# The first stage of a two-block model as one list of steps

## The chip, the cores and the metric

One core of a Trainium2 chip runs the whole program in one launch. The metric is the device time in microseconds. Before the change it is 3861.12 us, the median of three runs from 3858.9 to 3863.61. All data is fp32.

## What is computed

Two model blocks work on x of 256 rows by 2048. Block one is an attention layer and a Fourier layer, each behind a modulated layer norm; block two is a mixer, a cross-attention to a memory of 256 rows, and an expert layer with gathered rows. The change touches only the first stage, which prepares three things:

```
# modulation of layer 0, for the latents (c) and the context (c_ctx)
m = silu(cvec) @ ada_w[0] + ada_b[0]          # 2048 -> 6144; shift, scale, gate
h = layer_norm(x) * (1 + scale) + shift        # for x with c, for ctx with c_ctx
# keys and values of the memory
mem_n = rms_norm(mem, mem_norm_g)
kv = mem_n @ w_kv_mem                          # 2048 -> 4096: 2048 keys, 2048 values
```

Shift and scale, the first 4096 columns, are needed in this stage; the gate's columns come later. h of x and of ctx then goes into attention's input product (`z = h @ w_in`), whose first part is called z_q. Keys and values wait in DRAM for the second block.

## The kernel before, in words

Each engine has its own generator of instructions: `sp_mem`, `pe_mem`, `v_mem`, `a_mem` for the first stage (SP issues the loads, PE is TensorE, v is VectorE or DVE, a is ScalarE or ACT), then `sp_attention` and so on. Weights come through a ring of eight units of 1 MiB (`sp_slot`): a load waits until what was in its unit has been used. Beside its main work a program has a side list; `aside` (L98) takes steps from it at a rate, after each chunk of weights. SP, PE, DVE and ACT must take side steps at the same places, since they are written to meet there.

The order before is this. Constants arrive, ACT and DVE compute S5 phases (`a_phases`, `v_phases`), while POOL builds tables from them all the way to 723 us. Memory's rows are normed, turned by PE (L602) and evicted as columns by DVE (L621) and ACT (L637). Then the key blocks run (`pe_cols`, L354: four blocks of 512 columns, 16 k-steps of 128 each, plain fp32), and the value blocks (`pe_rows`, L331: plain fp32, 512 wide). Beside them run, at 3.2 steps for a chunk of eight k-steps, eight modulation blocks of 512 columns (`v_modulation`). For each of the 16 k-steps and each of the two vectors, DVE multiplies a row block of `ada_w` by a scalar of each partition and adds it up (L814); PE then sums over partitions with 8 matmuls against a column of ones (L841), and DVE adds the bias (L823). There is one pair of sums, `macc`: the next block can't begin until PE has read it, and DVE waits for that at L823 in its own order. Last come x and ctx, from the ring: DVE computes row moments (L690) and DVE and ACT norm one tile of 128 rows each (L697, L706); PE turns the rows in four parts of four k-steps (L602); DVE and ACT evict with scale and shift (L623, L639), ACT makes the high part (L441) and DVE the low part (L447).

Attention's products are split products in fp32r: a weight is a high part plus a low part, and so is the input; three fp32r matmuls (L470, L471, L472) stand for one fp32 matmul. For each k-step ACT copies the high part of the weights (L419) and DVE subtracts for the low one (L431), into four buffers (`BUFS`), which lie in the ring's last two units; `sp_parts` takes these from the ring and `a_parts` waits for them. In `split`, ACT and DVE are three k-steps ahead of the eviction and the side steps of a k-step. Behind the first stage the side list is the row modulation, the other 16 blocks (L874, L877).

Of the kernel before, what the change touches and what calls it, by code (L numbers as in the profile page):

```python
# [13 lines left out]
P = 128  # L14
# [357 lines left out]


def v_rows_out(c, L, tiles, dst):

    for b, (n, w) in enumerate(L.blocks):
        for _ in L.chunks[:-1]:
            yield from c.v.aside()
        for q, t in enumerate(tiles):
            if (b * len(tiles) + q) % 2 == 0:  # L380
                key = (L.name, n, t)
                yield from v_copy_out(c, key, dst(t, n, w), lambda: c.bank[key][:, 0:w])
        yield from c.v.aside()


def a_rows_out(c, L, tiles, dst):
    for b, (n, w) in enumerate(L.blocks):
        for _ in L.chunks[:-1]:
            yield from c.a.aside()
        for q, t in enumerate(tiles):  # L390
            if (b * len(tiles) + q) % 2:
                key = (L.name, n, t)
                yield from a_copy_out(c, key, dst(t, n, w), lambda: c.bank[key][:, 0:w])
        yield from c.a.aside()
# [186 lines left out]
def first_load(L):  # L581
    return (L.name, L.n0, 0)
# [198 lines left out]
def mod_load(layer, n, ch):  # L781
    return ("ada", layer, n, ch)


def sp_modulation(c, layer, blocks):
    W = c.I["ada_w"][layer]
    for n in blocks:
        for ch in range(2):
            yield from sp_load(c, mod_load(layer, n, ch),
                               W[ch * 8 * P:(ch + 1) * 8 * P, n:n + 512].rearrange("(k p) n -> p k n", p=P), 8, 512)  # L790
            yield True
            yield True
        yield True


def v_modulation(c, layer, blocks, who):
    nc, v = c.nc, c.v
    for n in blocks:
        for kk in range(KD):
            load = mod_load(layer, n, kk // 8)  # L800
            if kk % 8 == 0:
                yield from v.wait_ge(("in", load))
                wt = c.slot(load, 8, 512)
            elif kk % 4 == 0:
                yield True
            for w in range(who):
                acc, cv = c.macc[:, w, :], c.cv[:, w, kk:kk + 1]
                names = [("macc", layer, n, kk, w)]
                names += [("used", load)] if kk % 8 == 7 and w == who - 1 else []
                if kk == 0:  # L810
                    nc.vector.tensor_scalar(acc, wt[:, 0, :], cv, None, ALU.mult).then_inc(c.v_mod.after(*names), 1)
                else:
                    yield from v.wait_ge(("macc", layer, n, kk - 1, w))
                    nc.vector.scalar_tensor_tensor(out=acc, in0=wt[:, kk % 8, :], scalar=cv, in1=acc, op0=ALU.mult,  # L814
                                                   op1=ALU.add).then_inc(c.v_mod.after(*names), 1)
            if kk % 8 == 7:
                yield True
        key = ("mod", layer, n)
        yield from v.wait_ge(("full", key))
        j = n // P  # L820
        m = c.mod[:, layer, j:j + 4, 0:who]
        scale = D <= n < 2 * D
        nc.vector.tensor_tensor(m, c.bank[key][:, 0:4 * who].rearrange("p (a b) -> p a b", b=who),  # L823
                                c.col("ada_b%d" % layer)[:, j:j + 4].unsqueeze(2).broadcast_to([P, 4, who]),
                                ALU.add).then_inc(c.v_mod.after(("free", key), *([] if scale else [key])), 1)
        if scale:
            yield from v.wait_ge(c.v_mod)
            nc.vector.tensor_scalar(m, m, 1.0, None, ALU.add).then_inc(c.v_mod.after(key), 1)
        yield True


def pe_modulation(c, layer, blocks, who):
    for n in blocks:
        for _ in range(4):
            yield True
        key = ("mod", layer, n)
        bank = yield from pe_bank(c, c.aux, key)
        yield from c.pe.wait_ge(*[("macc", layer, n, KD - 1, w) for w in range(who)])
        for j in range(4):
            for w in range(who):  # L840
                mm = c.nc.tensor.matmul(bank[:, j * who + w:j * who + w + 1], c.macc[:, w, j * P:(j + 1) * P],  # L841
                                        c.ones[:, 0:1], start=True, stop=True)
        mm.then_inc(c.pe_full.after(("full", key)), 1)
        yield True


# [184 lines left out]

def mem_lins(c):
    W = c.I["w_kv_mem_2"][0]
    return Lin("mem_k", W, 0, D), Lin("mem_v", W, D, 2 * D)


def mem_views(c):
    return c.at(16 * K1, KD, SEQ), c.at(20 * K1, NT, D), c.at(24 * K1, KD, SEQ)


MOD0A = range(0, 2 * D, 512)
MOD0B = range(2 * D, 3 * D, 512)
MOD1 = range(0, 3 * D, 512)
INPUTS = (("x", 0), ("ctx", 1))
# [12 lines left out]

def pe_mem(c):
    pe = c.pe
    LK, LV = mem_lins(c)  # L1060
    KT, VV, memT = mem_views(c)
    mem = c.ring[:, 0, :].rearrange("p (t d) -> p t d", t=NT)
    yield from pe.wait_ge(("const", "rope"))
    yield from pe_turn(c, "mem", lambda k, t: mem[:, t, k * P:(k + 1) * P], KD, NT, normed("mem"))
    c.moments[("used", "mem")] = c.moments[("full", turn_banks("mem", KD, NT)[-1][0])]
    pe.side, pe.rate = [pe_modulation(c, 0, MOD0A, 2)] + [pe_input(c, name) for name, _ in INPUTS], 3.2
    yield from pe.wait_ge(*turn_free("mem", KD, NT))
# [6 lines left out]
def v_cols_out(c, L, dst, beside=True):  # L1074

    for n, w in L.blocks:
        if beside:
            for _ in L.chunks[:-1]:
                yield from c.v.aside()
        for j in range(0, w // P, 4):  # L1080
            key = (L.name, n, j)
            yield from v_copy_out(c, key, dst((n - L.n0) // P + j), lambda: pairs(c.bank[key][:, :]))
        if beside:
            yield from c.v.aside()


def a_cols_out(c, L, dst, beside=True):
    for n, w in L.blocks:
        if beside:
            for _ in L.chunks[:-1]:  # L1090
                yield from c.a.aside()
        for j in range(2, w // P, 4):
            key = (L.name, n, j)
            yield from a_copy_out(c, key, dst((n - L.n0) // P + j), lambda: pairs(c.bank[key][:, :]))
        if beside:
            yield from c.a.aside()


def v_mem(c):
    v = c.v  # L1100
    LK, LV = mem_lins(c)
    KT, VV, memT = mem_views(c)
    mem = c.ring[:, 0, :].rearrange("p (t d) -> p t d", t=NT)
    yield from v.wait_ge(("const", "rope"))
    yield from v_phases(c)
    yield from v.wait_ge(("in", "mem"))
    yield from v_rms(c, "mem", ("mem", "squares"))
    v_rms_rows(c, "mem", lambda t: mem[:, t, :], lambda t: mem[:, t, :])
    yield from v_turn_out(c, "mem", lambda k: memT[:, k, :], KD, NT, gain=lambda k: c.col("memn_g", k))
    yield from v.wait_ge(("mem", "silu"))  # L1110
    v.side, v.rate = [v_modulation(c, 0, MOD0A, 2)] + [v_input(c, name, w) for name, w in INPUTS], 3.2
    yield from v_cols_out(c, LK, lambda j: KT[:, j:j + 2, :])
    yield from v_rows_out(c, LV, range(NT), lambda t, n, w: VV[:, t, n - D:n - D + w])
    yield from v.aside(0)
    v.side = [v_row_modulation(c)]
# [28 lines left out]
def sp_input(c, name):  # L1144
    yield from sp_load(c, ("rows", name), c.I[name][0].rearrange("(t p) d -> p t d", p=P), NT, D)
    yield True
    for _ in range(4):
        yield True
# [1910 lines left out]
```

## Time and profile before

| | us |
|---|---|
| median of the runs | 3861.12 |
| the profiled execution, time | 3859.63 |
| its span | 3858.3 |
| busy PE / DVE / ACT / POOL | 2783.1 / 2677.6 / 1011.8 / 1491.3 |
| first matmul of the keys / of z_q | 28.10 / 334.61 |

PE is TensorE's matmuls, PEld its weight loads, DVE VectorE, ACT ScalarE, POOL GpSimd, SP the queue that issues the loads. A line number is that of the instruction, often a helper's. "Idle before" is the time that an engine stood still ahead of an instruction, and "<-" names what it waited for. The granted clock (PEclk) is TensorE's, with 1.00 for 2.4 GHz. A plain fp32 matmul appears as two records.

### The profile page before, as it was taken

What the parts mean: (1) busy time and instruction counts of PE and PEld (TensorE: products, weight loads), DVE (VectorE), ACT (ScalarE), POOL (GpSimd) and SP (SyncE); (2) the same over time, 40 slices, a digit from 0 to 9 for tenths busy, and PEclk for the clock granted to TensorE, in tenths of its full rate; (3) what the DMA queues carried; (4) which work ended last, traced back from release to release, by engine and by line L of the source; (5) the groups of instructions that cost most, each with busy time, mean ns of one, the idle gap of its engine ahead of it and who ended that gap; (6) DMA issues with size and microseconds to landing.
All of it is one profiled execution on the core that took longest, in us unless ns stands there. A gap on an engine that the chain in (4) does not pass through costs nothing.

```text
span 3858.3 us, 34052 instructions
## 1 busy us (share of the span) xinstructions
PE 2783.1 (72%) x12628; PEld 2060.6 (53%) x12628; DVE 2677.6 (69%) x3883; ACT 1011.8 (26%) x1884; POOL 1491.3 (39%) x1943
## 2 busy tenths in 40 slices
PE   7897989878799998979997897832434444444445
PEld 6645888546688975859876796730111111111112
DVE  6766867786654432657884554679888878888775
ACT  1013334123444421444465543410000000000000
POOL 7887877300000000000000000047776767777664
PEclk9888999999899999989998998865676766676678
DMA  8767666745455520544212451369999999999998
GB/s 295 267 240 250 222 241 213 254 137 182 153 192 187 184 88 22 187 173 164 99 66 92 159 219 66 134 255 405 417 421 422 421 421 411 417 421 419 420 422 343
DMA packets 284166, 974.23 MB, mean 253 GB/s; under 512 B 13408, under 2 KB 29664, under 8 KB 214752
## 3 DMA queue, kind: packets, MB, share of 16 engines
q0 software_dynamic: 76592, 551.58, 34.7%
q1 hardware_dynamic: 206000, 413.79, 30.4%
q10 hardware_dynamic: 1408, 6.69, 0.4%
q8 instruction: 99, 1.62, 0.2%
q14 instruction: 67, 0.55, 0.0%
HBM read 957.33 MB, written 14.68 MB: 252 GB/s over the span
## 4 chain that ended last, share of the span: by engine, by line
PE 53%; DVE 19%; DMA 15%; POOL 7%; issue 3%; ACT 3%; SPq 0%; DVEq 0%; ACTq 0%
DMA ring<-in_peer_v,arena 11%; POOL ring L2926 7%; PE lin L470 6%; PE lin L471 6%; PE lin L472 6%; PE lin L505 5%; PE lin L2690 5%; PE lin L508 5%; PE lin L507 5%; DVE mod_sums L877 3%; DMA ring<-in_peer_u,arena 3%; PE lin L2103 3%; DVE mod_sums L814 2%; PE lin L354 2%; DVE ring L2847 2%
## 5 line engine op out<-in xcount | busy, mean ns | idle before, releaser
L2690 PE MATMUL lin<-ring,diag 128*128 128x512 f32 x768 | 531.7, 857 | 738.7 <-DMA ring<-in_peer_v,arena 572.4
L431 DVE TENSOR_TENSOR weight_parts<-ring,weight_parts 128x512 fp32r<-128x512 f32 (+2 forms) x1010 | 660.9, 672 | 491.1 <-ACT weight_parts L419 489.4
L419 ACT CAST weight_parts<-ring 128x512 fp32r<-128x512 f32 (+2 forms) x1010 | 596.3, 598 | 748.5 <-PE lin L472 421.7
L2690 PEld LDWEIGHTS lin<-ring,diag 128*128 128x128 f32 x768 | 206.2, 282 | 1059.3 <-issue 883.2
L2847 DVE CUSTOM_DVE_ANT_0 ring<-ring,arena 128x2048 f32<-128x2048 f32 x256 | 583.4, 2289 | 156.8 <-DMA ring<-in_peer_u,arena 148.5
L2926 POOL DMA_INDIRECT ring<-in_peer_u,arena x256 | 458.9, 1793 | 421.8 <-DVE arena L2781 273.3
L2926 POOL DMA_INDIRECT ring<-in_peer_v,arena x256 | 467.7, 1827 | 234.9 <-PE lin L2690 161.6
L470 PE MATMUL lin<-weight_parts,parts 128*128 128x512 f32 (+2 forms) x1252 | 483.2, 386 | 57.6 <-DVE weight_parts L431 55.9
L2451 POOL DMA_DIRECT2D arena<-mem_values x1 | 0.6, 567 | 1347.5 <-PE lin L508 1347.5
L505 PE MATMUL lin<-parts,weight_parts 128*128 128x256 f32 x1600 | 465.7, 291 | 52.5 <-DVE weight_parts L431 52.5
L471 PE MATMUL lin<-weight_parts,parts 128*128 128x512 f32 (+2 forms) x1252 | 479.2, 383 | 0.0
L472 PE MATMUL lin<-weight_parts,parts 128*128 128x512 f32 (+2 forms) x1252 | 478.4, 382 | 0.0
L508 PE MATMUL lin<-parts,weight_parts 128*128 128x256 f32 x1600 | 461.0, 288 | 0.0
L507 PE MATMUL lin<-parts,weight_parts 128*128 128x256 f32 x1600 | 461.0, 288 | 0.0
L2835 DVE SCALAR_TENSOR_TENSOR arena<-ring,arena 128x2048 f32<-128x2048 f32 x160 | 375.9, 2349 | 49.4 <-DMA ring<-in_peer_v,arena 47.0
L505 PEld LDWEIGHTS lin<-parts,weight_parts 128*128 128x128 f32 x1600 | 316.2, 198 | 60.7 <-DVE weight_parts L431 54.7
L507 PEld LDWEIGHTS lin<-parts,weight_parts 128*128 128x128 f32 x1600 | 316.2, 198 | 0.1
L508 PEld LDWEIGHTS lin<-parts,weight_parts 128*128 128x128 f32 x1600 | 315.6, 197 | 0.0
L470 PEld LDWEIGHTS lin<-weight_parts,parts 128*128 128x128 f32 x1252 | 239.8, 192 | 110.4 <-DVE weight_parts L431 56.6
L472 PEld LDWEIGHTS lin<-weight_parts,parts 128*128 128x128 f32 x1252 | 239.6, 191 | 44.8
L471 PEld LDWEIGHTS lin<-weight_parts,parts 128*128 128x128 f32 x1252 | 239.7, 191 | 43.4
L2900 ACT ACTIVATE diag<-ident,arena 128x128 f32<-128x128 f32 x96 | 35.0, 394 | 609.3 <-PE lin L2690 489.8
(274 smaller groups left out, 3561.2 us busy)
## 6 DMA issues: line engine op xcount, KB each, us to landing
ring<-in_ada_w SPq DMA_DIRECT2D x64, 1024.0 KB, 6.5
ring<-in_w_in_fourier SPq DMA_DIRECT2D x32, 2048.0 KB, 8.0
ring<-in_w_kv_mem SPq DMA_DIRECT2D x16, 2048.0 KB, 10.9
ring<-in_ada_w SPq DMA_DIRECT2D x16, 2048.0 KB, 8.1
ring<-in_w_in_attn SPq DMA_DIRECT2D x32, 1024.0 KB, 6.9
ring<-in_w_out_fourier SPq DMA_DIRECT2D x16, 2048.0 KB, 8.0
ring<-in_w_in SPq DMA_DIRECT2D x24, 1024.0 KB, 5.1
ring<-in_w_out_attn SPq DMA_DIRECT2D x8, 2048.0 KB, 7.9
```

The source lines that it names most:

```text
L419: c.nc.scalar.copy(c.w_parts[:, q, 0, 0:w], c.slot(load, L.kc, w)[:, k % L.kc, :]).then_inc(c.a_high.after(("high", L.name, i)), 1)
L431: c.nc.vector.tensor_tensor(c.w_parts[:, q, 1, 0:w], c.slot(load, L.kc, w)[:, k % L.kc, :], c.w_parts[:, q, 0, 0:w].bitcast(F32), ALU.subt ...
L470: c.nc.tensor.matmul(banks[t][:, 0:w], lhs(0, k, t), hi, start=(k == 0), stop=False)
L471: c.nc.tensor.matmul(banks[t][:, 0:w], lhs(0, k, t), lo, start=False, stop=False)
L472: mm = c.nc.tensor.matmul(banks[t][:, 0:w], lhs(1, k, t), hi, start=False, stop=(k == L.K - 1))
L505: c.nc.tensor.matmul(o, hi[:, b], rhs(0, k), start=(k == 0 and j % 2 == 0), stop=False, skip_group_check=True)
L507: c.nc.tensor.matmul(o, hi[:, b], rhs(1, k), start=False, stop=False, skip_group_check=True)
L508: mm = c.nc.tensor.matmul(o, lo[:, b], rhs(0, k), start=False, stop=(k == L.K - 1), skip_group_check=True)
L2690: mm = nc.tensor.matmul(X.sums[t][b][:, :], c.diag[:, X.diag_of(t, k), :], X.bufs[gather_buf(n)][:, b * 512:(b + 1) * 512], start=(k == PE ...
L2835: nc.vector.scalar_tensor_tensor(out=X.H[:, t, :], in0=X.bufs[gather_buf(n)], scalar=X.act[:, t, k:k + 1], in1=X.H[:, t, :], op0=ALU.mult, ...
L2847: c.nc.vector.tensor_tensor_reduce(out=buf, in0=buf, in1=X.hn[:, t, :], scale=1.0, scalar=0.0, op0=ALU.mult, op1=ALU.add, accum_out=X.act[ ...
L2926: c.nc.gpsimd.indirect_dma_start(X.bufs[q], None, X.tables[table], bass.IndirectOffsetOnAxis(ap=X.idx[:, t, k:k + 1], axis=0)).then_inc(go ...
```

## The change

The side work of the first stage becomes one list, `beside_memory`, of 45 steps, which all four engines walk. There are 32 modulation steps (4 blocks of 1024 columns, each in 8 loads of two k-steps, 1 MiB), two norms (x behind the 16th modulation step, ctx behind the last), two pauses for the last sums, eight input parts and an end. There are two pairs of sums, and PE reads a pair two steps after its last addition, DVE adds the bias three steps after. The four additions of a step alternate between the two vectors, as before. Three steps are taken ahead of the keys (DVE one ahead of memory's rms, two behind it), 1.44 a chunk of four k-steps in the keys and 1.25 in the values. ACT takes over all evictions of keys, values and inputs and all of the inputs' normalising; DVE keeps the row moments and the low parts. Memory's values become split products; their input parts are made from memory's columns, the high part in other space and the low part in place, so DVE waits for the last key block. x's rows are loaded by SP ahead of the keys, ctx's rows by ACT's queue when the keys are stored, both into the arena and not the ring. The values leave in four stores of a block each. `sp_parts` and `a_parts` move ahead of the values. DVE's phases and ACT's first activation wait only for the first constants, whose order changes, and ACT's silu comes ahead of the phases.

```diff
-    return Lin("mem_k", W, 0, D), Lin("mem_v", W, D, 2 * D)
+    return Lin("mem_k", W, 0, D, kc=4, rate=1.44), Lin("mem_v", W, D, 2 * D, kc=4, every=4, rate=1.25)
...
+        self.KT = c.at(16 * K1, KD, SEQ)
+        self.T, self.T_flat = c.at(24 * K1, KD, SEQ), c.at(24 * K1, KD * SEQ)
+        self.parts = [c.at_r(20 * K1, KD * SEQ), c.at_r(24 * K1, KD * SEQ)]
+        self.V = c.at(28 * K1, 2, NT, 512)
+        self.x = [c.at(8 * K1, NT, D), c.at(16 * K1, NT, D)]
+        self.sums = [c.at((12 + 2 * i) * K1, 2, MOD_WIDTH) for i in range(2)]
...
+    steps = [("mod", b, q) for b in range(2 * D // MOD_WIDTH) for q in range(KD // 2)]
+    steps.insert(16, ("norm", 0))
+    steps += [("norm", 1), ("sum",), ("sum",)] + [("part", w, q) for w in range(2) for q in range(4)] + [("last",)]
...
+def v_beside(c):
+    nc, v, X, steps = c.nc, c.v, c.mem_in, beside_memory()
+    due, low = mod_due(steps, 3), None
...
+            yield from v.wait_ge(("in", load))
+            wt = c.slot(load, 2, MOD_WIDTH)
+            for k in range(2):
+                for w in range(2):
...
+                    else:
+                        yield from v.wait_ge(("sum0", b, q - (k == 0), 1 - k, w))
+                        nc.vector.scalar_tensor_tensor(out=acc, in0=wt[:, k, :], scalar=cv, in1=acc, op0=ALU.mult,
+                                                       op1=ALU.add).then_inc(c.v_mod.after(*names), 1)
+        if s[0] == "norm":
+            yield from v_input_norm(c, s[1])
...
+        if i in due:
+            yield from v_modulated_both(c, due[i])
+        yield True
...
+def a_beside(c):
...
+        if s == ("mod", 3, 3):
+            yield from a.wait_ge(("memk", "stored"))
+            nc.scalar.dma_start(X.x[1], c.I["ctx"][0].rearrange("(t p) d -> p t d", p=P)).then_inc(
+                Signal(c, "ctx_rows_in", 16).after(("rows", "ctx")), 16)
+        if s[0] == "norm":
+            w, name = s[1], INPUTS[s[1]]
+            yield from a_rstd(c, name, st_tmp(c, NT))
+            yield from a.wait_ge(("bias", name))
...
 def sp_mem(c):
...
-    sp.side, sp.rate = [sp_modulation(c, 0, MOD0A)] + [sp_input(c, name) for name, _ in INPUTS], 3.2
+    sp.side = [sp_beside(c)]
+    yield from sp.aside(3)
+    c.nc.sync.dma_start(c.mem_in.x[0], c.I["x"][0].rearrange("(t p) d -> p t d", p=P)).then_inc(
+        Signal(c, "x_rows_in", 16).after(("rows", "x")), 16)
+    sp.owed = 0.0
     yield from sp_weights(c, LK)
+    sp_parts(c)
     yield from sp_weights(c, LV)
...
 def pe_mem(c):
...
-    yield from pe_cols(c, LK, lambda k: memT[:, k, :])
-    yield from pe_rows(c, LV, lambda k, t: memT[:, k, t * P:(t + 1) * P], range(NT))
+    pe.side, pe.owed = [pe_beside(c)], 0.0
+    yield from pe.aside(3)
+    begin(pe, LK)
+    yield from pe_cols(c, LK, lambda k: X.T[:, k, :])
+    yield from pe_split_rows(c, LV, ("mem",), X.lhs)
...
 def v_mem(c):
...
+    yield from v_phases(c)
+    yield from v.wait_ge(("mem", "silu"))
+    v.side, v.owed = [v_beside(c)], 0.0
+    yield from v.aside(1)
...
+    yield from v.aside(2)
+    begin(v, LK)
+    for _ in LK.blocks:
+        for _ in LK.chunks:
+            yield from v.aside()
+
+    def x_part(q):
+        yield from v.wait_ge(("full", (LK.name, LK.blocks[-1][0], 2)))
+        yield from v_low_of_x(c, "mem", q, X.T_flat, *X.parts)
+
+    yield from v_split(c, LV, x_part, nothing)
...
 def a_mem(c):
...
+    yield from a_parts(c, first_load(LV))
+    yield from a_split(c, LV, None, out)
```

## Rows read from the trace of the kernel before

**Rows 1.** The page: its chain of waits by engine, whole span.

```profile
PE 53%; DVE 19%; DMA 15%; POOL 7%; issue 3%; ACT 3%; SPq 0%; DVEq 0%; ACTq 0%
```

**Rows 2.** Stretches: us, busy of each engine (instructions), PEclk, DMA share, GB/s.

```profile
28.00:335.00 307.00, 263.55 (x961) 179.55 (x962) 215.42 (x343) 29.14 (x46) 246.85 (x628) 0.90 0.67 244
```

**Rows 3.** Who waited for whom, 0 to 335 us: total us, times, longest.

```profile
DVE mod L823 <- PE aux L841: 30.7, 8, 7.9
...
PE aux L841 <- DVE mod_sums L814: 24.9, 5, 9.6
...
PE aux L602 <- DVE ring L697: 11.8, 1, 11.8
```

**Rows 4.** The PE's timeline: start, us, what, count, idle before it.

```profile
28.10 27.86 PE L354 MATMUL lin<-arena,ring 128*128 128x256 f32 x128 [1.13 <-ACT arena L637]
...
110.56 3.54 PE L841 MATMUL aux<-ones,mod_sums 128*128 128x1 f32 x16 [9.59 <-DVE mod_sums L814]
113.97 29.95 PE L354 MATMUL lin<-arena,ring 128*128 128x256 f32 x128
...
279.28 2.87 PE L602 MATMUL aux<-ident,ring 128*128 128x128 f32 x24
281.98 13.90 PE L331 MATMUL lin<-ring,arena 128*128 128x512 f32 x32
...
334.61 0.79 PE L470 MATMUL lin<-weight_parts,parts 128*128 128x512 f32 x1 [6.57 <-DVE weight_parts L431]
335.20 0.63 PE L471 MATMUL lin<-weight_parts,parts 128*128 128x512 f32 x1
335.62 0.63 PE L472 MATMUL lin<-weight_parts,parts 128*128 128x512 f32 x1
...
344.32 0.39 PE L471 MATMUL lin<-weight_parts,parts 128*128 128x512 f32 x1
344.55 0.39 PE L472 MATMUL lin<-weight_parts,parts 128*128 128x512 f32 x1
```

**Rows 5.** The DVE's timeline.

```profile
17.37 0.16 DVE L731 TENSOR_REDUCE st<-square_sums 128x2 f32<-128x8 f32 x1 [4.59 <-ACT squares_out L717]
...
204.68 19.96 DVE L814 SCALAR_TENSOR_TENSOR mod_sums<-ring,silu_c,mod_sums 128x512 f32<-128x512 f32 x30
...
263.06 4.83 DVE L690 BATCH_NORM_STATS2 bn<-ring 128x6 f32<-128x512 f32 x8
...
282.92 1.23 DVE L447 TENSOR_TENSOR parts<-arena,parts 128x1024 fp32r<-128x1024 f32 x1 [2.00 <-ACT parts L441]
...
333.77 2.71 DVE L431 TENSOR_TENSOR weight_parts<-ring,weight_parts 128x512 fp32r<-128x512 f32 x4
```

**Rows 6.** ACT's timeline.

```profile
282.79 1.01 ACT L639 ACTIVATE arena<-aux,mod 128x256 f32<-128x256 f32 x2
...
307.53 2.93 ACT L706 ACTIVATE ring<-ring,st 128x512 f32<-128x512 f32 x4 [1.43 <-DVE st L693]
...
331.55 1.04 ACT L441 CAST parts<-arena 128x1024 fp32r<-128x1024 f32 x1 [1.28 <-DVE arena L623]
...
337.62 0.62 ACT L419 CAST weight_parts<-ring 128x512 fp32r<-128x512 f32 x1 [2.51 <-PE lin L472]
```

**Rows 7.** Costliest groups by shape: busy us, mean ns, idle before.

```profile
L2835 DVE SCALAR_TENSOR_TENSOR arena<-ring,arena 128x2048 f32<-128x2048 f32 x160 | 375.9, 2349 | 49.4 <-DMA ring<-in_peer_v,arena 47.0
...
L1455 DVE TENSOR_TENSOR arena<-arena 128x1024 f32<-128x1024 f32 x2 | 3.0, 1490 | 0.1
```

**Rows 8.** Stretches under load, columns as in rows 2.

```profile
350.00:360.00 10.00, 10.00 (x49) 8.41 (x48) 9.51 (x16) 4.25 (x9) 3.56 (x13) 1.00 1.05 374
360.00:370.00 10.00, 7.42 (x60) 7.01 (x58) 8.40 (x17) 4.63 (x12) 8.74 (x25) 1.00 0.93 314
```

**Rows 9.** DMA issues of the first 340 us: count, KB each, median us to landing.

```profile
mem_keys<-arena ACTq DMA_DIRECT2D x1, 2048.0 KB, 11.6
```

**Rows 10.** POOL's timeline, first stage over.

```profile
894.48 0.72 POOL L1754 DMA_DIRECT2D arena<-in_x  x1 [170.85 <-DVE arena L1548]
```

More of the change, by code:

```diff
@@ L775, in pe_spread @@
         yield True
[L781 to L829, printed above, removed]
@@ L832, in pe_modulation @@
[L832 to L844, printed above, removed]
@@ new lines, in pe_beside @@
+def pe_beside(c):
+    X, steps = c.mem_in, beside_memory()
+    due = mod_due(steps, 2)
+    for i, s in enumerate(steps):
+        if i in due:
+            b = due[i]
+            key = ("mod0", b)
+            bank = yield from pe_bank(c, c.aux, key)
+            yield from c.pe.wait_ge(("sums", b))
+            for j in range(MOD_WIDTH // P):
+                for w in range(2):
+                    mm = c.nc.tensor.matmul(bank[:, 2 * j + w:2 * j + w + 1], X.sums[b % 2][:, w, j * P:(j + 1) * P],
+                                            c.ones[:, 0:1], start=True, stop=True)
+            mm.then_inc(c.pe_full.after(("full", key)), 1)
+        if s[0] == "part":
+            _, w, q = s
+            name = INPUTS[w]
+            yield from pe_turn(c, (name, q), lambda k, t: X.x[w][:, t, (4 * q + k) * P:(4 * q + k + 1) * P], 4, NT,
+                               lambda k: normed(name)(4 * q + k))
+        yield True
@@ new lines, in v_input_norm @@
+def v_input_norm(c, w):
+    name, X = INPUTS[w], c.mem_in
+    yield from c.v.wait_ge(("rows", name), ("normed", "x" if w else "mem", 1, D - 512))
+    for t in range(NT):
+        for j in range(4):
+            ins = c.nc.vector.bn_stats(c.bn[:, t, j, :], X.x[w][:, t, j * 512:(j + 1) * 512])
+    ins.then_inc(c.v_step.after(), 1)
+    yield from v_row_moments(c, name)
+    c.nc.vector.scalar_tensor_tensor(out=c.st[:, 40:42], in0=c.mv[:, :, 0], scalar=-1.0, in1=c.st[:, 0:2], op0=ALU.mult,
+                                     op1=ALU.mult).then_inc(c.v_step.after(("bias", name)), 1)
@@ L1058, in pe_mem @@
 def pe_mem(c):
-    pe = c.pe
+    pe, X = c.pe, c.mem_in
     LK, LV = mem_lins(c)
[L1061 to L1064, printed above, removed]
+    yield from pe.wait_ge(("const", "ident"))
+    yield from pe_turn(c, "mem", lambda k, t: X.rows[:, t, k * P:(k + 1) * P], KD, NT, normed("mem"))
     c.moments[("used", "mem")] = c.moments[("full", turn_banks("mem", KD, NT)[-1][0])]
-    pe.side, pe.rate = [pe_modulation(c, 0, MOD0A, 2)] + [pe_input(c, name) for name, _ in INPUTS], 3.2
@@ L1087, in a_cols_out @@
[L1087 to L1096, printed above, removed]
 def v_mem(c):
-    v = c.v
+    v, X = c.v, c.mem_in
     LK, LV = mem_lins(c)
-    KT, VV, memT = mem_views(c)
-    mem = c.ring[:, 0, :].rearrange("p (t d) -> p t d", t=NT)
+    yield from v.wait_ge(("const", "colpack"), ("const", "ident"))
@@ L1127, in a_mem @@
     yield from a.wait_ge(("in", "mem"))
[L1128 removed]
+    yield from a_row_squares(c, "mem", lambda t: X.rows[:, t, :])
     yield from a_rstd(c, "mem", st_tmp(c, NT))
[L1130 to L1133 removed]
@@ new lines, in a_mem @@
+    yield from a_turn_out(c, "mem", lambda k: X.T[:, k, :], KD, NT, gain=lambda k: c.col("memn_g", k))
+    yield from a.wait_ge(("const", "ident"), ("const", "rope"))
+    a.side, a.owed = [a_beside(c)], 0.0
+    yield from a.aside(3)
+    yield from a.wait_ge(*turn_free("mem", KD, NT))
+    for q in range(4):
+        a_high_of_x(c, "mem", q, X.T_flat, X.parts[0])
+    begin(a, LK)
+    for n, w in LK.blocks:
+        for _ in LK.chunks[:-1]:
+            yield from a.aside()
+        for j in range(0, w // P, 2):
+            key = (LK.name, n, j)
+            yield from a_copy_out(c, key, X.KT[:, n // P + j:n // P + j + 2, :], lambda: pairs(c.bank[key][:, :]))
+        yield from a.aside()
@@ new lines, in a_mem, with out @@
+    yield from a.wait_ge(*cols_free(LK))
+    nc.scalar.dma_start(c.memk, X.KT).then_inc(Signal(c, "mem_keys_stored", 16).after(("memk", "stored")), 16)
+    stored = [Signal(c, f"mem_values_stored{i}", 16) for i in range(2)]
+    def out(b):
+        n, w = LV.blocks[b]
+        yield from a.wait_ge(("memv", b - 2) if b > 1 else None)
+        for t in range(NT):
+            key = (LV.name, n, t)
+            yield from a_copy_out(c, key, X.V[:, b % 2, t, :], lambda: c.bank[key][:, :])
+        yield from a.wait_ge(*[("free", (LV.name, n, t)) for t in range(NT)])
+        nc.scalar.dma_start(c.memv[:, :, n - D:n - D + w], X.V[:, b % 2, :, :]).then_inc(
+            stored[b % 2].after(("memv", b)), 16)
@@ L1624, in a_attention @@
     a.owed = 0.0
-    yield from a_parts(c, first_load(X.z_q))
     yield from a_jobs(c, [
```

186 lines of the change are left out of this document (80 added, 106 removed).

## The prediction

> **What bounds the kernel now.** I read the chain of waits first, whole [rows 1], then its part before 335 us, then the table of stretches, the waits and each engine's own timeline there. Over the whole span PE holds 53% of the chain and DVE 19%. The change touches only what lies before the first matmul of the attention input product (z_q), at 334.61 us [rows 4]. From the end of memory's transposes, at 28 us, that stage lasts 307 us, with PE busy 263.6, DVE 215.4, ACT 29.1, the DMA engines 67% busy and the clock at 0.90 of full [rows 2]. So no engine is full. PE and DVE wait for each other: the modulation sums have one buffer, so PE waits 24.9 us for them and DVE 30.7 us until PE has read them [rows 3]; PE waits 11.8 us for ctx's layer norm [rows 3] and 6.57 us for the first split weights [rows 4]. Two costs are of another kind: memory's values in plain fp32, and the lost clock.
>
> **Unit costs.** A key block is 64 fp32 matmuls (two records each) in 27.86 us [rows 4]. A value matmul, 512 wide, takes 13.90 / 16 = 0.87 us [rows 4], 111 us for 128 of them. An fp32r matmul of 512 starts every 0.43 us at the half clock (335.20 to 335.62) and every 0.227 at the full one (344.32, 344.55) [rows 4]: a k-step of six takes 1.36 us, all 64 take 87 us. Eight transposes take 2.87 / 3 = 0.96; eight modulation matmuls took 3.54 us behind a gap of 9.59 and must be about half that at the full clock [rows 4]. DVE's product-and-add of 512 takes 19.96 / 30 = 0.665 [rows 5]. For 1024, no row of before: twice 0.665 is 1.33; the 2048-wide row gives 2.349 / 2 = 1.17; the dearest 1024-wide row of two tensors 1.49 [rows 7]; the cast difference of 1024 takes 1.23 [rows 5]. I take 1.20, near the last and on the line between 512 and 2048 (0.665 + 512 more elements at 1.1 ns), and keep 1.17 and 1.49. A modulation step (one 1 MiB load, four instructions) is then 4.8 us. DVE's low part of weights takes 2.71 / 4 = 0.68, of inputs 1.23, eight bn_stats 4.83 [rows 5]. ACT: high part of weights 0.62, of inputs 1.04, four normalised pieces 2.93, two evicted transposes 1.01 [rows 6].
>
> **The sum.** *Head.* The constants' order brings DVE's phase work under a us forward, off the path. The first modulation step goes into DVE's idle 4.59 us before memory's rms [rows 5], but its load lands after memory's rows, so it starts near 14 and ends near 19, where the rms began at 17.37. I charge 1.2 us: the keys start at 29.3 instead of 28.1. SP now puts three ada loads and x's rows ahead of the first key load, 8 MiB in all; at 374 GB/s [rows 8] they take 22.4 us from about 5, landing near 28, so just hidden.
>
> *Keys.* PE: 4 x 27.86 = 111.4, and two modulation blocks of 16 matmuls, 3.5 each: 118.4, so to 147.7. The step rate 1.44 over 16 chunks is 23 steps, behind 3 in front. DVE has no evictions left (ACT takes them; it is idle 90%) and does, from 28.7, 24 modulation steps (115.2), x's statistics (4.83 + about 2.2 for the root: 7.0) and two additions (0.5): to 151.4. DMA: 16 chunks and 22 ada loads of 1 MiB from 32 us, 39.8 MB, or 106 us at 374. All three are close; DVE is last by 4 us.
>
> *Values, first 24 k-steps.* DVE must make the lows of memory's transposes after the keys, because they are written over them: 4 x 1.23 = 4.9; 24 lows of weights 16.3; the last seven modulation steps 33.6; an addition 0.4: 55.2, to 206.6. PE needs 32.7 of it: it waits in each modulation step, whose 4.8 us is longer than the three k-steps (4.1) it has ready.
>
> *Turn to ctx.* Four more lows (2.7), ctx's statistics (7.0), during which ACT waits for the root, then ACT's eight normalised pieces, since DVE no longer shares them (5.9), one high and one low (1.3): the next k-step (31) can start at 223.5. PE has run dry for some 10 us, which brings the half clock back: the block behind the 9.59 us gap took 29.95 against 27.86 [rows 4], and its eight modulation matmuls lost about as much, so I charge 2.5. Ctx's rows are loaded by ACT after the keys are stored; two transfers of 2 MiB at 11.6 us [rows 9] from about 150 and 178 end before 206.
>
> *Rest.* PE, 33 k-steps 44.9; 64 transposes 7.7; one modulation block 3.5; the clock 2.5; refills where ACT does two parts and an eviction at once, 4: to 286.1. An input part on ACT (2.0 + 1.04) with high and low behind it is 4.4 us, against 5.1 that PE has in hand: hidden. At the seam ACT must evict the last value block before it splits z_q's first weights: 4 us, z_q at 290.
>
> That is 44.6 us before 334.61. Behind it nothing waits for a fixed time: POOL is through with its phases 170.85 us before its next work, which waits for attention at 894 [rows 10], now near 850. Attention starts with a fuller ring (PE idled in 360 to 370 [rows 8]), worth perhaps 3 us; against it, it shares 45 us more with POOL's phases, which I put at 2. The profiled execution took 3859.63 us (span 3858.3) and so comes to about 3815; the median of the runs, 3861.12, lies 1.5 above it: **3816**.
>
> **A rule weighed.** In rows 350 to 360 all transfers are 1 MiB with strips of 2 KB, and run at 374 GB/s with the DMA engines full [rows 8]. The Trainium skill (DMA: Bandwidth & Descriptors, Bandwidth) speaks against halving every load: it gives about 2 us fixed per transfer beside 436 GB/s. By that rule, were the transfers taken one by one, 64 loads of 1 MiB at 4.4 us and three of 2 MiB at 6.8 would put z_q near 307 as an estimate; the trace disagrees, since the fixed part lies under the neighbours' transfers in these rows.
>
> **The rivals.**
> - *Four buffers don't carry the values.* Each of the 16 pauses of ACT and DVE may cost PE a refill of high, low and signal, 1.4 us, not only those I charged; or the ring of six units runs dry (314 GB/s in 360 to 370 with PE idle 2.6 us [rows 8]). 16 x 1.4 = 22: 3838. For it: ACT waited 2.51 for PE at z_q's start [rows 6]. Against: it caught up in the stretch behind.
> - *Small transfers keep the rate down.* The stage's loads are 70 MiB, 73.4 MB. At the 244 GB/s that it moves now [rows 2] they take 301 us, and z_q starts near 310: 3835. Against: the 374 above; the 244 is what was asked for.
> - *1024-wide sums at 1.49 us* [rows 7]: 0.29 x 124 = 36 more, on the path nearly everywhere: 3852.
> - *PE sets the pace throughout* because DVE's sums at 1.17 and its waits hide: values 87 + 7.7 + 5 + 4 from 150, z_q near 258: 3784. Against: 55 us of DVE's work after the keys.
> - *Slower: the half clock stays.* The values' matmuls run in bursts between DVE's steps. At 0.43 us, 64 k-steps take 164 us: the first 24 need 61.5 (8 over DVE), the other 40 take 48 more, the transposes 8, less the 2.5 charged: z_q near 352, 3878. It decides when some 28 of the 40 late k-steps run at the half clock. For it: 0.90 in the stage now [rows 2]. Against: at 344 the full clock was back some 5 us after the gap [rows 4], and the late k-steps are dense. The Trainium skill (TensorE: Matmul & The Clock Gate, HAM oscillation) describes bursts that pay the low clock each time.
> - *No change:* the time gained is given back in attention, which starts bound by DMA. Against: 374 GB/s is what it gets now too.
>
> **Chances.** Forecast 0.60 (alone 3803 to 3830); refills 0.12; small transfers 0.03; dear sums 0.05; PE's pace 0.08; half clock 0.06; no change 0.06 (half of it a small loss). A difference of under 0.2%, 8 us, can't be told from none. Faster 0.86, same 0.06, slower 0.08. Low end 3792, between the forecast and PE's pace; high end 3848, past the refills and near the dear sums.
>
> **What would show it.** Product-and-add of 1024 at 1.2 us (128 of them); the keys' first matmul near 29.3; keys' end near 150; DVE without a gap from 29 to 210, PE with gaps of 1 to 3 us from 150 to 207 and one of 10 at ctx's norm; z_q near 290; everything behind it shifted by 40 to 50. Wrong: sums waiting for ada loads, PE at the half clock for most of the values, or a z_q that is early and an attention that ends where it did.

## The result

| | before | after |
|---|---|---|
| median of 7 runs each, us | 3861.12 (3852.91 to 3863.61) | 3832.68 (3817.33 to 3841.1) |
| ratio after/before, 95% interval | | 0.992 [0.9906, 0.9934] |
| profiled execution: time / span, us | 3859.63 / 3858.3 | 3831.52 / 3830.1 |
| first matmul of the keys / of z_q | 28.10 / 334.61 | 27.00 / 303.69 |
| from z_q to the span's end | 3523.7 | 3526.4 |

The change gains 28.4 us. The forecast was 3816 us; the time is inside its range, with 63% of the gain that it expected (45). All of the gain is there at z_q (30.9 us), and nothing behind z_q adds to it.

### The profile page after: what moved, and what is told of

The parts are those of the page before. It is cut to its first block, busy times and chain, and to the rows that moved or that the text cites. A ratio compares the mean times of both kernels' runs of the same rounds, so it can differ in the third digit from the quotient of the medians.

```text
span 3830.1 us, 34385 instructions
## 1 busy us (share of the span) xinstructions
PE 2770.9 (72%) x12756; PEld 2090.5 (55%) x12756; DVE 2689.8 (70%) x3785; ACT 1070.4 (28%) x1984; POOL 1536.5 (40%) x1943
## 4 chain that ended last, share of the span: by engine, by line
PE 40%; POOL 24%; DMA 16%; DVE 11%; issue 7%; ACT 2%; ACTq 0%; DVEq 0%; POOLq 0%
DMA ring<-in_peer_v,arena 10%; POOL ring L2940 8%; PE lin L448 5%; PE lin L450 5%; PE lin L449 5%; PE lin L2704 4%; PE lin L483 4%; PE lin L485 4%; PE lin L486 4%; DMA ring<-in_peer_u,arena 3%; PE lin L2117 3%; DMA phases<-phase 2%; DVE ring L2861 2%; POOL phase L933 2%; POOL phase_products L930 2%
## 5 line engine op out<-in xcount | busy, mean ns | idle before, releaser
L409 DVE TENSOR_TENSOR weight_parts<-ring,weight_parts 128x512 fp32r<-128x512 f32 (+2 forms) x1074 | 702.0, 673 | 533.2 <-ACT weight_parts L397 531.6
L397 ACT CAST weight_parts<-ring 128x512 fp32r<-128x512 f32 (+2 forms) x1074 | 633.8, 599 | 806.4 <-PE lin L450 469.0
L2940 POOL DMA_INDIRECT ring<-in_peer_u,arena x256 | 442.5, 1728 | 426.0 <-DVE arena L2795 273.5
L448 PE MATMUL lin<-weight_parts,parts 128*128 128x512 f32 (+2 forms) x1380 | 539.7, 391 | 89.0 <-DVE weight_parts L409 87.3
L449 PE MATMUL lin<-weight_parts,parts 128*128 128x512 f32 (+2 forms) x1380 | 532.1, 386 | 0.0
L450 PE MATMUL lin<-weight_parts,parts 128*128 128x512 f32 (+2 forms) x1380 | 531.8, 385 | 0.0
L448 PEld LDWEIGHTS lin<-weight_parts,parts 128*128 128x128 f32 x1380 | 266.0, 193 | 151.8 <-DVE weight_parts L409 87.5
L450 PEld LDWEIGHTS lin<-weight_parts,parts 128*128 128x128 f32 x1380 | 265.3, 192 | 50.7
L449 PEld LDWEIGHTS lin<-weight_parts,parts 128*128 128x128 f32 x1380 | 266.3, 193 | 48.4
```

Source lines behind the costliest of these rows:

```text
L397: c.nc.scalar.copy(c.w_parts[:, q, 0, 0:w], c.slot(load, L.kc, w)[:, k % L.kc, :]).then_inc(c.a_high.after(("high", L.name, i)), 1)
L409: c.nc.vector.tensor_tensor(c.w_parts[:, q, 1, 0:w], c.slot(load, L.kc, w)[:, k % L.kc, :], c.w_parts[:, q, 0, 0:w].bitcast(F32), ALU.subt ...
L448: c.nc.tensor.matmul(banks[t][:, 0:w], lhs(0, k, t), hi, start=(k == 0), stop=False)
L449: c.nc.tensor.matmul(banks[t][:, 0:w], lhs(0, k, t), lo, start=False, stop=False)
L450: mm = c.nc.tensor.matmul(banks[t][:, 0:w], lhs(1, k, t), hi, start=False, stop=(k == L.K - 1))
L2940: c.nc.gpsimd.indirect_dma_start(X.bufs[q], None, X.tables[table], bass.IndirectOffsetOnAxis(ap=X.idx[:, t, k:k + 1], axis=0)).then_inc(go ...
```

## The profile after

In the changed kernel the key matmuls are L355 and the modulation's L1004 (16 in a block, two records each). The split products are L448 to L450 (six matmuls, or 1.36 us, for each step of 128 rows, a k-step), the low parts of weights and inputs L409 and L425 on DVE, the high parts L397 and L419 on ACT. The sums are L1033, the statistics L1064, the bias L1050, ACT's normalising L1085.

The stage first, as in [rows 2], then five pieces of it (same columns).

```profile
28.00:335.00 307.00, 270.55 (x1233) 228.50 (x1232) 243.45 (x280) 98.25 (x170) 258.26 (x460) 0.92 0.74 271
66.00:70.00 4.00, 4.00 (x10) 3.18 (x10) 4.00 (x4) 0.00 (x0) 3.92 (x3) 0.50 1.03 394
114.00:119.00 5.00, 5.00 (x15) 4.10 (x15) 5.00 (x6) 0.00 (x0) 4.76 (x5) 0.50 0.63 248
230.00:246.00 16.00, 15.46 (x54) 13.60 (x55) 3.96 (x8) 4.28 (x8) 11.61 (x57) 0.52 0.55 190
```

DVE went from 215 to 243 us of work in these 307 and ACT from 29 to 98. The clock hardly rose (0.90 to 0.92), and the next rows say where it is lost: TensorE is busy for all of 66 to 70 and of 114 to 119, and has only the half clock there. Who waited for whom up to 335 us, as in [rows 3]:

```profile
ACT weight_parts L397 <- PE lin L450: 57.7, 44, 8.9
DVE weight_parts L409 <- ACT weight_parts L397: 48.0, 28, 6.3
PE lin L448 <- DVE weight_parts L409: 36.4, 10, 10.1
ACT weight_parts L397 <- DMA ring<-in_w_kv_mem: 10.8, 3, 8.6
```

The waits of [rows 3] for sums (24.9), for their reading (30.7, now one of 7.8 further down) and for ctx's norm (11.8) are gone; in their place PE waits 36.4 us for DVE's low parts, 10.1 of them while ctx is normed. TensorE's timeline, as in [rows 4]:

```profile
27.00 34.77 PE L355 MATMUL lin<-arena,ring 128*128 128x256 f32 x160 [1.39 <-DMA ring<-in_w_kv_mem]
61.61 4.20 PE L1004 MATMUL aux<-ones,arena 128*128 128x1 f32 x32
65.67 44.47 PE L355 MATMUL lin<-arena,ring 128*128 128x256 f32 x192
109.98 4.72 PE L1004 MATMUL aux<-ones,arena 128*128 128x1 f32 x32
114.56 37.02 PE L355 MATMUL lin<-arena,ring 128*128 128x256 f32 x160
...
200.11 0.80 PE L448 MATMUL lin<-weight_parts,parts 128*128 128x512 f32 x1 [6.98 <-DVE weight_parts L409]
...
230.54 0.79 PE L448 MATMUL lin<-weight_parts,parts 128*128 128x512 f32 x1 [10.12 <-DVE weight_parts L409]
...
233.27 6.82 PE L1004 MATMUL aux<-ones,arena 128*128 128x1 f32 x32
...
303.69 0.80 PE L448 MATMUL lin<-weight_parts,parts 128*128 128x512 f32 x1 [4.61 <-DVE weight_parts L409]
```

The first 160 records of the keys run at the full clock (34.77 us); the last 160, behind a modulation block, take 37.02. Nowhere in the keys does PE wait. DVE's timeline, as in [rows 5]:

```profile
26.00 34.62 DVE L1033 SCALAR_TENSOR_TENSOR arena<-ring,silu_c,arena 128x1024 f32<-128x1024 f32 x28
...
146.01 2.47 DVE L1033 SCALAR_TENSOR_TENSOR arena<-ring,silu_c,arena 128x1024 f32<-128x1024 f32 x2
151.62 1.23 DVE L425 TENSOR_TENSOR parts<-arena,parts 128x1024 fp32r<-128x1024 f32 x1 [3.14 <-PE lin L355]
...
187.95 1.94 DVE L409 TENSOR_TENSOR weight_parts<-ring,weight_parts 128x512 fp32r<-128x512 f32 x3 [3.30 <-ACT weight_parts L397]
...
209.17 4.87 DVE L1033 SCALAR_TENSOR_TENSOR arena<-ring,silu_c,arena 128x1024 f32<-128x1024 f32 x4
216.36 4.84 DVE L1064 BATCH_NORM_STATS2 bn<-arena 128x6 f32<-128x512 f32 x8
...
240.12 0.17 DVE L1050 TENSOR_TENSOR mod<-aux,colpack_sb 128x16 f32<-128x16 f32 x1 [7.83 <-PE aux L1004]
```

A sum of 1024 takes 1.22 us (4.87 / 4), and up to 148.5 DVE has no pause but one of 0.27. The 3.30 us at 187.95 are ACT's in truth, as its own timeline says:

```profile
187.30 1.66 ACT L397 CAST weight_parts<-ring 128x512 fp32r<-128x512 f32 x3 [8.59 <-DMA ring<-in_w_kv_mem]
...
223.51 5.75 ACT L1085 ACTIVATE arena<-arena,st 128x512 f32<-128x512 f32 x8 [1.46 <-DVE st L1067]
```

One view misleads. The page's chain of waits by engine, as in [rows 1], and POOL's x load, as in [rows 10]:

```profile
PE 40%; POOL 24%; DMA 16%; DVE 11%; issue 7%; ACT 2%; ACTq 0%; DVEq 0%; POOLq 0%
```

```profile
868.31 0.72 POOL L1768 DMA_DIRECT2D arena<-in_x  x1 [83.74 <-DVE arena L1563]
```

POOL is suddenly 24% of the chain, yet it had been done for 83.74 us when DVE released its x load. The chain was followed back through POOL's own earlier work; POOL set nothing here.

## The experiments

Each ratio is to the kernel before, timed on the same chip; its median there lay between 3861.12 and 3865.11 us, so compare the ratios and not the medians. "z_q" is z_q's first matmul in the profiled execution, one for each kernel. In the ten kernels with the changed head the keys began between 26.84 and 28.99 us, so a difference of a us or two at z_q can be the execution's.

| | median | ratio, 95% | keys' end | z_q |
|---|---|---|---|---|
| after | 3832.68 | 0.992 [0.9906, 0.9934] | 151.6 | 303.69 |
| e7 before, two pairs of sums | 3827.41 | 0.9904 [0.9887, 0.992] | 148.4 | 299.32 |
| e5 plain values | 3811.13 | 0.9866 [0.9849, 0.9882] | 148.6 | 278.66 |
| e11 plain values, ring of six | 3806.16 | 0.9846 [0.983, 0.9863] | 151.9 | 282.99 |
| e4 sums 512 wide | 3847.84 | 0.9964 [0.9952, 0.9977] | 156.7 | 323.30 |
| e9 plain values, sums 512 wide | 3816.64 | 0.9875 [0.9851, 0.9899] | 156.2 | 289.37 |
| e1 blocks of 8 | 3836.19 | 0.9912 [0.9888, 0.9936] | 144.7 | 300.50 |
| e2 ctx's norm spread | 3822.38 | 0.989 [0.9874, 0.9907] | 151.0 | 295.57 |
| e3 both of these | 3824.4 | 0.9897 [0.9881, 0.9914] | 145.9 | 294.86 |
| e8 plain values, blocks of 8 | 3800.36 | 0.9846 [0.9815, 0.9877] | 145.2 | 273.50 |
| e6 POOL's tables late | 3902.64 | 1.011 [1.0083, 1.0137] | 147.5 | 298.26 |

**The kernel before with two pairs of sums** (e7). Theory: the mutual wait is what the change removes; rival: the wider sums and ACT's work are needed too.

```diff
-                acc, cv = c.macc[:, w, :], c.cv[:, w, kk:kk + 1]
+                acc, cv = mod_sums(c, n)[:, w, :], c.cv[:, w, kk:kk + 1]
+def mod_sums(c, n):
+    return c.macc if n // 512 % 2 == 0 else c.at(12 * K1, 2, 512)
```

PE reads a pair two steps, and DVE adds the bias three steps, after the last sum.

> The kernel before, with one thing changed: two pairs of modulation sums of 512, PE reading a pair two side steps later and DVE adding the bias in the middle of the next block. Theory A: the mutual wait (PE 24.9 us for DVE, DVE 30.7 us for PE) is most of what the change takes away; PE's gaps of 5.7 to 9.6 us go and with them the half clock, z_q starts at 310 to 316 instead of 334.6, and the run is 18 to 25 us shorter. Rival B: the waits only move to the end of the stage, where x and ctx come, and less than 8 us are gained.

It gained 35.3 us at z_q, more than the whole change and more than the theory's 19 to 25. The wait for ctx's norm fell with the mutual wait, from 11.85 to 3.01. Two rows of TensorE's timeline: a block of 8 at the full clock, and the largest gap in the values.

```profile
132.63 1.84 PE L855 MATMUL aux<-ones,arena 128*128 128x1 f32 x16
...
167.88 16.36 PE L331 MATMUL lin<-ring,arena 128*128 128x512 f32 x32 [4.08 <-DMA ring<-in_w_kv_mem]
```

So the rival fell: this one part, without wider sums or ACT's work, gives more than the gain, and the rest of the change sums to 4.4 us lost at z_q.

**Memory's values in plain fp32** (e5). The split's parts, its four buffers and the lows of memory's columns go; the ring keeps eight units until z_q.

```diff
-    yield from pe_split_rows(c, LV, ("mem",), X.lhs)
+    yield from pe_rows(c, LV, lambda k, t: X.T[:, k, t * P:(t + 1) * P], range(NT))
```

> The changed kernel, with memory's values in plain fp32 matmuls as before the change, beside the same list of steps; no parts of memory's weights or columns are made, and the ring keeps eight units through the values. Theory A (DVE bounds the values' first part): the split saves PE 24 us of matmuls but puts 43 us of low parts on DVE and 4 buffers between; with plain products PE runs through from 151 with 111 us of values, 8 of transposes, 7 to 10 of modulation and a seam of 6, and z_q starts at 285 to 292, 12 to 18 us before 303.7. Rival B (the split pays as it does in the unit costs): z_q starts 15 to 25 us later than 303.7.

z_q came 25.0 us earlier, past the theory's 12 to 18, although each value k-step has 1.74 us of matmuls in place of 1.36. A stretch of it, columns as in [rows 2], and its TensorE:

```profile
150.00:210.00 60.00, 60.00 (x185) 30.16 (x184) 42.32 (x46) 8.30 (x13) 47.92 (x107) 1.00 1.03 390
```

```profile
148.46 7.03 PE L332 MATMUL lin<-ring,arena 128*128 128x512 f32 x16
155.33 3.63 PE L1004 MATMUL aux<-ones,arena 128*128 128x1 f32 x32
158.82 48.31 PE L332 MATMUL lin<-ring,arena 128*128 128x512 f32 x112
...
278.66 0.50 PE L448 MATMUL lin<-weight_parts,parts 128*128 128x512 f32 x1 [4.32 <-DVE weight_parts L409]
```

PE is busy for all 60 us and at the full clock, with DMA full at 390 GB/s beside it. So what the change adds to the two pairs of sums has two sides: without the split it brings z_q from 299.32 (e7) to 278.66, and the split takes 25.0 us back.

**The same with the ring at six units** (e11), since e5 had changed the ring too.

```diff
+    sp_parts(c)
     yield from sp_weights(c, LV)
```

> The kernel after with memory's values as plain fp32 matmuls, but with the ring kept at six units through the values (the earlier plain version had eight there). What it tells apart: whether the 25 us that the plain version gained at z_q came from the product itself or from the two more units of the ring. Theory A (the product: DVE's lows, ACT's highs and the four buffers between them and PE are gone): PE still runs with nearly no gap, z_q between 277 and 284 (278.66 with eight units). Rival B (the ring: PE eats a 1 MiB chunk of weights in 7.0 us, and with six units loads come late once DVE holds some): waits of PE for loads of w_kv_mem of 10 us or more together in 150 to 275, and z_q at 290 to 304. The total then stays within 8 us of the eight-unit version's 3811 under A, and near 3825 under B.

z_q at 282.99, 4.3 us later: the values start 3.3 later (1.6 of it stood already where the keys began, 28.99 against 27.39) and wait 2.5 for loads, and e5 had lost 1.7 to the half clock in them, which e11 did not. With the ring as it was, the product alone gives 20.7 of the 25 us; the two more units are worth some 4.

```profile
177.80 7.13 PE L332 MATMUL lin<-ring,arena 128*128 128x512 f32 x16 [1.73 <-DMA ring<-in_w_kv_mem]
185.71 27.70 PE L332 MATMUL lin<-ring,arena 128*128 128x512 f32 x64 [0.78 <-DMA ring<-in_w_kv_mem]
```

**Sums 512 wide again**, with split values (e4) and with plain ones (e9).

```diff
-                        nc.vector.scalar_tensor_tensor(out=acc, in0=wt[:, k, :], scalar=cv, in1=acc, ...)
+                        for h in range(2):
+                            o = slice(h * 512, h * 512 + 512)
+                            nc.vector.scalar_tensor_tensor(out=acc[:, o], in0=wt[:, k, o], scalar=cv, in1=acc[:, o], ...)
```

> The changed kernel, its sums in instructions of 512 instead of 1024 columns (two for each, same loads, same steps). Theory A (DVE bounds the stage from 26 to 214 us when the values are split): a step takes 8 x 0.665 = 5.3 us instead of 4.84, 31 steps 15 us more, and z_q starts 11 to 16 us after 303.7. Rival B (PE sets the pace, the DVE has room): less than 3 us.

> The kernel with plain fp32 values (z_q at 278.7), its sums in instructions of 512. Theory A: without the low parts DVE is off the path, it was done with its sums at 191 and PE reads the last block at 207, so 15 us more on DVE still fit: z_q moves by less than 3 us. Rival B (DVE bounds the keys too, at 151 us): 5 to 15 us later, as in the kernel with split values.

The first addition of a block is cut in two in the same way. z_q moved by 19.6 us in e4, more than expected, and by 10.7 in e9, where the theory that DVE's time is hidden there fell. In both, PE waits in the keys for the first pair of sums, which it does in none of the versions with wide sums (e4):

```profile
67.54 6.99 PE L1004 MATMUL aux<-ones,arena 128*128 128x1 f32 x32 [5.36 <-DVE arena L1036]
```

With narrow sums DVE bounds the keys as well. In this order of the steps the wide sums are worth 11 to 20 us at z_q. The kernel with two pairs (e7) has narrow sums in the old order, and z_q at 299.32; what wide sums would give there wasn't tried.

**Blocks of 8 modulation matmuls** (e1), the second half one step later, and DVE's bias one step later too.

```diff
-            for j in range(MOD_WIDTH // P):
+            for j in range(0, 4) if first else range(4, 8):
```

> The changed kernel, with each block of 16 modulation matmuls cut into two of 8, one side step apart, and DVE's addition one step later. Theory A: the long block of one-column matmuls itself brings PE's clock down, with no idle time ahead of it (after the two blocks in the keys a stretch at the half clock stands, and the keys take 116.3 us of matmuls where 111.4 are their full pace). Then the keys' matmuls take about 111.5 us in three groups, the keys end near 147, DVE's 3.1 us wait for them goes, and z_q starts 4 to 7 us before 303.7. Rival B: the clock falls on its own rhythm or for the load of all engines; then the keys' matmuls still take 115 us or more and z_q moves by less than 1.5 us.

The keys took 117.9 us in place of 124.6, at the full clock throughout, and PE then waited 6.86 us for DVE. z_q gained 3.2 us, less than the theory's 4 to 7, and the total nothing that can be told.

**ctx's norm spread** (e2): ACT's eight pieces as four and four in the two pauses for the last sums.

```diff
-    steps += [("norm", 1), ("sum",), ("sum",)] +
+    steps += [("norm", 1), ("rest", 0), ("rest", 1)] +
```

> The changed kernel, with ctx's norm spread over three side steps: DVE's statistics in the first, ACT's eight normalised pieces four by four in the next two (they were pauses). Theory A: PE's gap of 10.1 us at 220 us is the sum of DVE's 7 us and ACT's 5.9 us one after the other, with four buffers of 4.1 us against it; apart they leave two gaps of 2 to 4 us, the half clock of 230 to 246 us goes, and z_q starts 7 to 10 us earlier. Rival B: the time comes back at the next wait because ACT has the same work ahead of the input parts; z_q moves by less than 3 us.

```profile
228.37 0.79 PE L448 MATMUL lin<-weight_parts,parts 128*128 128x512 f32 x1 [5.38 <-DVE weight_parts L409]
231.10 3.71 PE L1004 MATMUL aux<-ones,arena 128*128 128x1 f32 x32
```

The gap is 5.38 us and not 10.12, the block behind it 3.71 and not 6.82, and z_q 8.1 us earlier, as the theory said. Of that, 1.9 us came only behind a later wait of 2.8 us, equally long in both: the changed kernel ran at the half clock behind it, and e2 did not.

**Both edits together** (e3).

> The kernel after with both small edits together: each block of 16 one-column modulation matmuls cut into two of 8 one step apart, and ctx's norm spread over the pauses. Alone, the first brought z_q to 300.50 (-3.2) and the second to 295.57 (-8.1). Theory A (two separate costs: the half clock behind the blocks of 16, and ACT's norm as one step): z_q near 292 to 294, the matmuls at the full clock from the keys to the first gap, the gap before the last modulation block near 5 us, and the last two half blocks at 1.84 us each or, if they follow the gap, under 5 us together. Rival B (DVE bounds the stretch to 214 whatever PE's clock, so the cut blocks can only give what they give behind DVE's work): z_q stays within 1.5 us of 295.6, and the keys' earlier end turns into a longer wait for DVE.

z_q at 294.86, only 0.7 before e2 alone. That is the number of the rival, but its mechanism explains only a part of it. The keys ended 5.2 us before e2's, and PE then waited longer for DVE (6.80 us against 4.22), as the rival says. Yet behind ctx's gap PE resumed at 223.75, still 4.6 us before e2 (228.37). That lead went in the last modulation block, whose two halves met behind the gap and ran at the half clock: 6.82 us against 3.71, where under 5 had been expected. Why e2's block had the full clock there and this one did not wasn't tried, so that the two edits don't add up isn't shown to be DVE's doing.

```profile
152.66 0.76 PE L448 MATMUL lin<-weight_parts,parts 128*128 128x512 f32 x1 [6.80 <-DVE weight_parts L409]
...
223.75 0.66 PE L448 MATMUL lin<-weight_parts,parts 128*128 128x512 f32 x1 [4.95 <-DVE weight_parts L409]
...
226.34 6.82 PE L1008 MATMUL aux<-ones,arena 128*128 128x1 f32 x32
```

**Plain values and blocks of 8** (e8).

> Plain fp32 values and the modulation matmuls in blocks of 8. Theory A: now that PE bounds the stage, the half clock behind the blocks of 16 (2.6 us in the keys, about 2 behind the last block) is on the path: z_q starts 4 to 6 us before 278.7. Rival B: the time is hidden here too, within 1.5 us.

Here PE and not DVE bounds the stage, and the 5.2 us of the clock reach z_q, within the 4 to 6 expected. It has the lowest median, 3800.36 us, and its interval ends (0.9877) below the start of the changed kernel's (0.9906); it overlaps those of e5 and e11, so the three can't be put in order by their times.

**POOL's tables begun behind the values** (e6), to see what DVE and POOL do to each other.

```diff
-    yield from c.g.wait_ge(("const", "rope"))
+    yield from c.g.wait_ge(("const", "rope"), ("full", ("mem_v", 2 * D - 512, 1)))
```

> The changed kernel, with POOL's phase tables begun only when the last value block is done (298 us). Theory A (POOL and DVE slow each other): DVE's product-and-add of 1024 drops from 1.21 us to below 1.18, z_q starts 3 to 8 us earlier, and POOL, which needs about 550 to 600 us for its tables, ends near 870 to 900, where the load of x behind them at 868 becomes late by up to 30 us, which the run then shows. Rival B (only POOL is slowed, DVE goes first): the sums stay at 1.21 us and z_q within 2 us, and the run is later by what the load of x is late.

z_q came 5.4 us earlier, but that isn't shown to be POOL's. 4.1 us of it stood at the keys' end, where DVE waited for PE in both kernels: PE fell to the half clock behind one of the two blocks in the keys and not behind both. Another 1.9 came behind the same later wait as in e2, by the clock again. What shows POOL's part is the sums themselves. The two rows are DVE's sums from 26 to 215 us, after and then e6 (busy us, mean ns):

```profile
L1033 DVE SCALAR_TENSOR_TENSOR arena<-ring,silu_c,arena 128x1024 f32<-128x1024 f32 x118 | 146.1, 1308 | 0.0
```

```profile
L1033 DVE SCALAR_TENSOR_TENSOR arena<-ring,silu_c,arena 128x1024 f32<-128x1024 f32 x118 | 142.1, 1278 | 0.0
```

DVE lost about 3% to POOL; in the seven other kernels with wide sums this group takes 146.1 to 149.0 us. The sums did not fall under 1.18 us as theory A had it (142.1 / 118 = 1.20). The price came later and was more than twice the 30 us expected: the tables ended at 933 us, and the x load behind them held DVE.

```profile
DVE parts L425 <- DMA arena<-in_x: 69.4, 1, 69.4
```

## Why the forecast was right in kind and off in size

| step of the forecast | forecast | measured | adds |
|---|---|---|---|
| keys start | 29.3 | 27.0 | |
| keys' end | 151.4 | 151.6 | +0.2 |
| values' first 24 k-steps end | 206.6 | 214.0 | +7.2 |
| k-step 31 starts | 223.5 | 230.5 | -0.4 |
| values' end | 286.1 | 298.9 | +5.8 |
| z_q | 290 | 303.7 | +0.9 |
| z_q to the end, against before | -1 | +2.7 | +3.7 |

*Head.* 2.3 us too dear: the sums of the first step ran from 14.06 and pushed memory's rms by 0.4 us only (17.78 against 17.37), not by 1.2 or more. Some of the rest is the execution's, as the spread of the keys' start says.

*Keys.* The end was right by luck, by two errors against each other. The start was early, and PE, not DVE, was last: the forecast had 111.4 us of matmuls and two blocks of 3.5, the trace has 116.3 and 8.9, because the half clock came behind each block. With blocks of 8 (e1) PE needs 111.7 and DVE is last, as the forecast had it.

*Values, first 24 k-steps.* This step failed, by 7.2 of the 13.7 us at z_q. The sums were right (28 x 1.22 = 34.0 against 33.6). Missing were three things. DVE's waits were put at nothing and took 4.5 us: 3.30 for ACT, which stood 8.59 us for a load, and two of about 0.6 for ACT's highs. The forecast counted 24 lows of weights, but DVE runs three k-steps ahead and makes 27 before this point, 2.0 us more; its own next k-step is 31, which is 27 and the four lows of the turn. And a low took 0.71 on average (20.5 us for 29), not 0.68, another 0.8. The late load was issued at 175.47, when SP had stood 8.4 us until DVE gave a unit of the ring back. That is one half of the rival "four buffers don't carry the values", which had the mechanism at 22 us. No run has the split with a longer ring, so how much of it the ring of six costs isn't shown.

*Turn to ctx.* 16.5 us against 16.9. That ACT's normalising would set the gap was right, and e2 shows that its price (8.1 at z_q) was a choice of the change and not needed.

*Rest.* From k-step 31 to the values' end was the second step that failed, by 5.8. The charge for the half clock, 2.5, was read from one block of [rows 4] behind one gap. In the changed kernel the modulation block itself falls into it (6.82 us, not 3.5), DVE waits 7.83 for that block, and the clock is at 0.52 from 230 to 246.

*Seam.* From the values to z_q it was 4.8 us against 4.

*Behind z_q.* The 3 us for a fuller ring did not show. From z_q to the first scores took 421.8 us before and 422.9 after. From z_q to the span's end it was 3523.8 (e4) to 3541.1 (e1) in kernels that are the same there, so the 3.7 us of the last row can't be told from none.

*The rivals.* Small transfers: fell, the DMA reached 394 GB/s in 66 to 70 with PE busy throughout. Dear sums: fell, 1.22. PE's pace: fell, DVE set it from 151 to 214. Two sums slip among the rivals: the terms of PE's pace give 253.7 at z_q and not 258, and the half clock's 61.5 us are 6.3 over DVE's 55.2 and not 8. The half clock stays: it came and went again. No change: fell.

*What the forecast did not ask.* It priced the split values at 87 us of matmuls against 111 and never compared them with the plain product under its own finding that DVE holds the first 24 k-steps. Its own numbers said it: 24 plain k-steps are 41.8 us of PE, and without the lows DVE has 34, where the split ones have 32.7 of PE and 55.2 of DVE. It also named the mutual wait as a cost beside others, and did not say how much of the gain it alone would give; e7 says more than all of it.

*POOL.* The forecast put 2 us on sharing with POOL's tables. The last table was stored at 783.9 us and not 722.9, which took POOL's slack ahead of its x load from 170.85 [rows 10] to 83.74: no cost here, but e6 shows what it costs once the slack is gone. The same instruction on POOL, from 28 to 335 us, before and then after:

```profile
L1007 POOL TENSOR_TENSOR phase_tmp<-phase_tmp 128x2 f32<-128x2 f32 x49 | 17.4, 355 | 3.8
```

```profile
L919 POOL TENSOR_TENSOR phase_tmp<-phase_tmp 128x2 f32<-128x2 f32 x36 | 21.1, 586 | 2.8
```

These tiny operations went from 355 to 586 ns when DVE's instructions beside them became 1.22 us long and unbroken; another line of the same form went from 364 to 479. It is the length that counts: beside unbroken sums of 512 (e4) the two lines take 392 and 359 ns. The Trainium skill (SBUF — State Buffer, SBUF: two separate sides) has a rule for it: a DVE operation with two SBUF inputs and a GpSimd operation that reads SBUF exclude each other for a whole instruction. By that rule, the trace agrees in kind: the sums have two such inputs, and each side lost: POOL as above, DVE 146.1 us against 142.1 in e6.

*Left open.* From z_q to the first scores the same instructions took between 415.7 us (e8) and 433.2 (e11) in the profiled executions, at a mean granted clock of 0.97 and of 0.93. So a single profile is good to some 15 us behind z_q, and the order of e5 and e11, 3811 and 3806, says nothing. Why the clock differs there from one execution to the next wasn't tried.

## What to carry to other kernels

When two engines wait for each other over one buffer, try the second buffer alone before redesigning the stage: alone it gave 35.3 us at z_q, and the whole redesign 30.9. Before a product is split to save TensorE's time, add up the splitting work on the engine that would be last; with DVE the bound, the slower product was the faster kernel here. And read the bound again after each fix: with DVE and ACT last, the width of the sums and a norm in one piece are on the path.

## What the hardware did that was not expected

*The half clock without a wait.* Blocks of one-column modulation matmuls brought the half clock with no idle time ahead or behind. In the kernels of this study 23 blocks of 16 began at the full clock in an unbroken stretch of matmuls; behind 15 of them the granted clock went to 0.50, behind 8 it stayed at 1.00, and which of the four blocks it was differed from kernel to kernel. Behind 28 blocks of 8 in the same position, three of them in the kernel before, it never fell. A short wait ahead was enough to change that: behind the block of 8 at 201.66 in the kernel before, which had waited 0.56 us, it was at 0.50. The row of 114 to 119 us above is such a fall; the same stretch of e1, with a block of 8 in it:

```profile
114.00:119.00 5.00, 5.00 (x33) 4.61 (x32) 5.00 (x5) 0.59 (x1) 4.76 (x5) 1.00 0.80 258
```

The forecast had charged the half clock only behind gaps, as [rows 4] show it, and its cited section of the Trainium skill (TensorE: Matmul & The Clock Gate, HAM oscillation) tells of bursts with waits between them. That section has no case without a wait; the trace has one, and it costs 6.7 us in the keys (124.6 against 117.9 in e1).

*Loads overlap.* With PE and DVE both busy the stage's 1 MiB loads came at 390 GB/s for 60 us (e5), against 374 in [rows 8].
